# The second half of the up projection as seven block products in place of eight, for 8 of 11 column pairs, with the weight sums made in DRAM

## What is computed

```python
n2 = rmsnorm(h, ln2)
up = n2 @ w_up                      # 544 x 1024 by 1024 x 5632
u, vv = up[..., :D_FF], up[..., D_FF:]      # D_FF = 2816
uc, conv_tail = causal_dwconv(u, conv_prev, conv_w, conv_b)
h = h + (jax.nn.gelu(uc, approximate=False) * vv) @ w_down
```

## Time and profile before

| | before |
|---|---|
| time, median of 3 runs | 845.98 us (844.97 to 847.61) |
| the profiled execution: its time / its span | 846.78 / 844.7 us |
| busy: PE / DVE / ACT / POOL | 831.9 / 535.4 / 375.9 / 182.4 us |
| chain that ended last, share on PE | 93% |
| up loop on the chain | 453.3 to 712.6 us |

### The profile page before, as it was taken

One profiled execution on the slowest core, in us unless ns is written; L12 is line 12 of the kernel. 1 busy time (PEld: TensorE's weight loads), 2 busy tenths in 40 slices (PEclk: granted clock), 3 DMA queues, 4 the chain that ended last, 5 costly groups with the idle time before them and its releaser, 6 DMA issues.

```text
span 844.7 us, 16289 instructions
## 1 busy us (share of the span) xinstructions
PE 831.9 (98%) x6634; PEld 820.7 (97%) x6634; DVE 535.4 (63%) x671; ACT 375.9 (45%) x479; POOL 182.4 (22%) x224
## 2 busy tenths in 40 slices
PE   9999999999999999999999999999999999999996
PEld 8999999999999989999999999999999999999996
DVE  4464668486899876766555544545544555778973
ACT  5553234332455454543243533443443344644574
POOL 3017236343324200000400422222212122000020
PEclk9999999999999999999999999999999999999998
DMA  8769978982326993544892662232123323655522
GB/s 262 215 200 176 280 241 179 228 271 91 124 79 130 195 224 114 175 137 151 219 213 93 151 185 80 69 99 96 53 99 99 99 71 98 217 172 171 171 71 106
DMA packets 138526, 128.94 MB, mean 153 GB/s; under 512 B 5493, under 2 KB 130121, under 8 KB 138460
## 3 DMA queue, kind: packets, MB, share of 16 engines
q1 hardware_dynamic: 106636, 97.15, 37.1%
q0 software_dynamic: 31680, 30.55, 20.2%
q10 hardware_dynamic: 160, 0.53, 0.2%
HBM read 122.24 MB, written 41.62 MB: 194 GB/s over the span
## 4 chain that ended last, share of the span: by engine, by line
PE 93%; DVE 4%; ACT 1%; issue 1%; DMA 0%; DVEq 0%; SPq 0%; ACTq 0%
PE mm L1844 63%; PE mm L2235 8%; PE ax L1863 6%; PE ax L2235 6%; PE mm L2135 4%; PE ax L2135 3%; PE ax L1868 2%; DVE grs L1306 1%; DVE wlo L1296 1%; PE mm L1856 0%; ACT nhi L907 0%; DVE ylo L1541 0%; PE mm L1863 0%; DMA x_smp<-in_x_sample 0%; DVE wlo L1553 0%
## 5 line engine op out<-in xcount | busy, mean ns | idle before, releaser
L1844 PE MATMUL mm<-nhi,whi 128*128 128x272 f32 x1216 | 257.0, 293 | 0.9 <-DVE wlo L1296 0.6
L1844 PE MATMUL mm<-nhi,wlo 128*128 128x272 f32 x1216 | 252.8, 289 | 0.0
L1844 PE MATMUL mm<-nlo,whi 128*128 128x272 f32 x1216 | 251.8, 289 | 0.0
L1844 PEld LDWEIGHTS mm<-nhi,whi 128*128 128x128 f32 x1216 | 193.0, 190 | 3.5 <-issue 1.0
L1844 PEld LDWEIGHTS mm<-nlo,whi 128*128 128x128 f32 x1216 | 192.2, 190 | 0.0
L1844 PEld LDWEIGHTS mm<-nhi,wlo 128*128 128x128 f32 x1216 | 191.0, 190 | 0.0
L907 ACT ACTIVATE whi<-raw 128x2048 fp32r<-128x2048 f32 (+2 forms) x79 | 114.3, 1465 | 93.0 <-PE mm L1844 69.3
L1296 DVE TENSOR_TENSOR wlo<-raw,whi 128x2048 fp32r<-128x2048 f32 x44 | 103.7, 2356 | 28.7 <-ACT whi L907 28.6
L907 ACT ACTIVATE whi<-ring 128x1408 fp32r<-128x1408 f32 x25 | 34.6, 1383 | 44.1 <-PE ax L2235 24.0
L907 ACT ACT_TABLE_LOAD x22 | 28.2, 1283 | 58.3 <-DVE ext L1683 56.7
L2235 PE MATMUL mm<-bhi,whi 128*128 128x272 f32 x176 | 51.4, 292 | 0.0
(11 more groups left out here) (351 smaller groups left out, 1556.3 us busy)
## 6 DMA issues: line engine op xcount, KB each, us to landing
raw<-in_w_up SPq DMA_DIRECT2D x44, 512.0 KB, 4.4
raw<-in_w_in SPq DMA_DIRECT2D x36, 512.0 KB, 5.2
ring<-w_sums SPq DMA_DIRECT2D x16, 704.0 KB, 4.1
w_sums<-in_w_down SPq DMA_DIRECT2D x12, 704.0 KB, 11.4
w_sums<-in_w_down POOLq DMA_DIRECT2D x12, 704.0 KB, 16.7
ring<-in_w_down SPq DMA_DIRECT2D x9, 704.0 KB, 4.6
w_sums<-w_sums POOLq DMA_DIRECT2D x8, 704.0 KB, 9.5
g_sums<-in_w_in SPq DMA_DIRECT2D x18, 256.0 KB, 5.3
```

The costliest lines, as they stand in the source:

```text
L1844: ins = pe.matmul(mm[:, 2 * j + a, 0:HALF], w, x[:, kx, HALF * a:HALF * (a + 1)], start=first and n == 0 and m == 0, stop=last and n == le ...
```

## The change

Pairs 1 to 8 compute their v unit as `four` and `three`, seven block products in the four banks of `ax` (`UPS`, `UP_BLOCKS`); pairs 0, 9 and 10 stay as they were. The weight sums for it (`v_sums`, 256 KB a piece) are copied by SP in the last head units, where the copies for `w_sums` were, and added by POOL behind the head: 16 additions, 2 copies, 16 additions. SP waits for all of them before it loads the first `four`. The 12 copies for `w_sums` move to SP's loads of `w_o` and of u units 0 to 3, two at a time, and POOL's additions to the pauses behind pairs 0 to 7. The loops are written out. Token sums (`usum`, `uhigh`, `ulow`) are made around pairs 0 and 1. The last product takes its sign in the multiplication with the gelu. Two small shifts touch the gate units: in an `out` unit ACT copies `m_kept` of the next block before the second `mhi`, and `t_low(3)` comes after the second `mlo`.

The core of the diff:

```diff
+UPS = []
+for _i in range(KF // 2):
+    UPS += [("u", _i)] + ([("four", _i), ("three", _i)] if 1 <= _i <= 8 else [("v", _i)])
+U_DOWN = U_UP + len(UPS)
+UP_BLOCKS = range(1, 9)
...
+            if u >= 9:
+                i, block = gs_copies[(u - 9) // 2]
+                for n in range(1 + 4 * ((u - 9) % 2), 5 + 4 * ((u - 9) % 2)):
+                    sp.dma_start(v_sum(i, n), v_block(*block, n)).then_inc(vs_begun[i], 16)
...
+        for n, (kind, i) in enumerate(UPS):
+            u = U_UP + n
+            if kind in ("u", "v"):
+                load(u % 2, u - 1, *cols(w_up, UC * i + (D_FF if kind == "v" else 0)))
             else:
+                if i == 1:
+                    for k in (G_1, G_2, G_3) if kind == "four" else (G_4,):
+                        sp.wait_ge(vs_done[k], 16 * len(UP_BLOCKS))
+                block_load(u, kind, w_up, D_FF + UC * i, v_sums[:, i - 1])
+            if kind == "u" and i < 4:
+                begin_sums(2 + i)
...
+        for i in range(KF // 2):
             up_pair(i)
+            if i < 2:
+                weight_sum(S_3, (2 * i, 2 * i + 1), (0, 1))
+            elif i < 4:
+                weight_sum(S_1, (2 * i - 4, 2 * i - 3), (1, 1))
+            elif i < 6:
+                if i == 4:
+                    pool.wait_ge(sum_done[S_3], 16 * MD)
+                    for m in range(MD):
+                        pool.dma_start(w_sums[S_2, :, m], w_sums[S_3, :, m]).then_inc(sum_begun[S_2], 16)
+                else:
+                    weight_sum(S_2, (0, 1), (1, 1))
+            elif i == 6:
+                weight_sum(S_2, (2, 3), (1, 1))
+            elif i == 7:
+                pool.wait_ge(sum_done[S_2], 16 * MD)
+                weight_sum(S_4, range(MD), S_2)
...
+        for k in range(4):
+            run(tile(usum[0], k), resid[:, k, HALVES[1]], ACT.Copy, t_first, scale=vec(V_LN2 + k))
+        for i in range(KF // 2):
...
+                if j == 1 and i in UP_BLOCKS:
+                    keep(gact[:, 2 * i, HALVES[0]], ax, b, 0)
                 if j == 1:
...
+                    next_hi(x)
+                if j == 1 and i in UP_BLOCKS:
+                    keep(gact[:, 2 * i + 1, HALVES[1]], ax, b, 1)
...
+        make_sums(usum, V_LN2, 0)
         inverse(rstd[:, :], "rstd2", rstd_ready)
...
+            if kind in ("u", "v"):
                 for j in range(2):
...
+            elif kind == "four":
+                if i == 1:
+                    aux_wait_drained(pe, "rstd2")
+                four(u, up_block(i), ax, uhigh, ulow, 4)
+            else:
+                three(u, up_block(i), ax, uhigh, ulow, 4)
```

More of the change, by code:

```diff
@@ L432, in build @@
     silu_done, y_prod, y_hi, y_lo = map(sem, ("silu_done", "y_prod", "y_hi", "y_lo"))
+    vs_begun = [sem(f"vs_begun{i}") for i in range(4)]
+    vs_done = [sem(f"vs_done{i}") for i in range(4)]
     gs_begun = [sem(f"gs_begun{i}") for i in range(4)]
@@ L508, in flat, with gate_kind, first_piece @@
         return t[:, :, :].rearrange("p k c -> p (k c)")
+    def gate_kind(u):
+        return GATES[u - U_GATE][0] if U_GATE <= u < U_WO else UPS[u - U_UP][0] if U_UP <= u < U_DOWN else None
+    PIECED = [u for u in range(U_BLOCK, U_DOWN) if u < U_WO or gate_kind(u) in ("four", "three")
+              or gate_kind(u) and gate_kind(u - 2) == "four"]
     def pieces(u):
-        return (slice(0, 512), slice(512, 1536)) if GATES[u - U_GATE][0] == "three" else (slice(0, 1024), slice(1024, 2048))
+        return (slice(0, 512), slice(512, 1536)) if gate_kind(u) == "three" else (slice(0, 1024), slice(1024, 2048))
+    def first_piece(u):
+        return PIECED.index(u) + 1
     def blocks(g, q):
@@ L1118, in _ @@
                         next_hi(u)
+                        if q < 3:
+                            keep(m_kept[:, :], ax, blocks(0, q + 1)[1], 0)
                     act.wait_ge(m_sum, 2 * q + j + 1)
@@ L1127, in _ @@
                     act.wait_ge(block_added, 4 * blocks(g, q)[1] - 1)
-                keep(m_kept, g, q, 0)
+                    keep(m_kept[:, :], (ax, mm)[g], blocks(g, q)[1], 0)
                 if g == 0:
@@ L1596, in _ @@
                         dve.wait_ge(s0r_out[i], 32)
-                    make_sums(0)
-                    make_sums(1)
+                    make_sums(tsum, V_LN1, 0)
+                    make_sums(tsum, V_LN1, 1)
                     next_lo(u)
                 else:
-                    t_low(0)
-                    t_low(1)
+                    t_low(tsum, tlow, thigh, 0)
+                    t_low(tsum, tlow, thigh, 1)
             elif kind == "out":
@@ L1612, in _ @@
                             next_lo(u - 1)
-                        if q == 0 and b == 1 and j == 1:
-                            t_low(3)
                         dve.tensor_tensor(halves(mx[b][:, :]), slot(b), halves(gsig[:, 2 * b + j, :]), ALU.mult
@@ L1621, in _ @@
                     dve.tensor_tensor(mlo[:, m, :], mx[0][:, :], mhi[:, m, :].bitcast(F32), ALU.subtract).then_inc(m_lo, 1)
-                    if q == 0 and j == 0:
-                        t_low(2)
+                    if q == 0:
+                        t_low(tsum, tlow, thigh, 2 + j)
                 next_lo(u)
@@ L1714, in up_pair @@
-            u = U_UP + 1
-            lo(u + 2, u % 2, i * 2 + (u + 3))
-        with dve.Fori(0, KH // 2 + 1) as i:
+                        k = i * 2 - KH - 1
+                        third(gact[:, k:k + 2, HALVES[0]], gact[:, i * 2 - 1:i * 2 + 1, HALVES[0]])
+            next_lo(x + (2 if blocked else 1))
+            if i == 0:
+                make_sums(usum, V_LN2, 3)
+                t_low(usum, ulow, uhigh, 0)
+        for i in range(KF // 2):
             up_pair(i)
-        st.n -= 6
@@ L2112, in _, with block_product @@
                           done=filled_sem(s) if j == NJ - 1 else None)
-        def block_product(u, g, q, product, first, step, xh, xl):
-            n, b = blocks(g, q)
+        def block_product(u, b, bank_of, product, first, step, xh, xl):
             s = u % 2
             start = product not in (2, 4, 6)
-            if b >= 2 and product == 0:
-                pe.wait_ge(block_kept, 3 * (b - 2) + 3)
-            elif b >= 2 and start:
-                pe.wait_ge(block_added, 4 * (b - 2) + {1: 2, 3: 4, 5: 3}[product])
+            last = b - 2 if b < 6 else b - 1
+            if start and last >= 0:
+                pe.wait_ge(block_kept, 3 * last + 3)
+                if product:
+                    pe.wait_ge(block_added, 4 * last + {1: 2, 3: 4, 5: 3}[product])
             if product == 2:
@@ L2129, in block_product @@
                 pe.wait_ge(block_added, 4 * b + 1)
-            out = (ax, mm)[g][:, BLOCK_BANKS[product], 0:HALF]
+            out = bank_of[:, BLOCK_BANKS[product], 0:HALF]
             for k in range(4):
```

402 lines of the change are left out of this document (242 added, 160 removed).

## The result

| | before | after |
|---|---|---|
| time, median | 845.98 us (844.86 to 849.31, 7 runs) | 850.03 us (849.48 to 853.11, 7 runs) |
| ratio to before | | 1.0046, 95% interval 1.0033 to 1.0059 |
| the profiled execution: its time / its span | 846.78 / 844.7 us | 849.79 / 848.0 us |

The change makes the kernel slower by 4 us, where 842 us was forecast; the time lies inside the range of 836 to 851, on the wrong side of the kernel before.

A forecast was written before the change was run, and what follows sets the result against it. PE was taken to bound the kernel. From 846.78 us, -12.0 matmuls, -1.6 `m_kept`, +6.4 start, +2.0 loads and +1.0 gates gave 842.6, stated as 842 for the median; range 836 to 851.

The forecast's parts named there:

- The matmuls, -12.0: Up loop: eight pairs lose 12 matmuls each, 96 at 0.1252 us, 12.0 us less.
- The start, +6.4: Start of the up loop: four new waits of PE, 1.5, 1.5, 2.1 and 1.3 us, together 6.4, bounds 4.5 to 8.
- the start costs nothing: Rival, start of the up loop: the sums hide behind matmuls after all, giving 835.5 us; chance 0.12.
- A steady pair, at nothing: Block pairs of the up loop: PE's 22.5 us hide the other engines' work, cost zero; `keep` has half a microsecond left.
- `m_kept`, -1.6: Gates, first block's third product: the earlier copy removes PE's 2.0 us wait; gain 1.6 us, between 0 and 2.0.
- The gates ... 1.0 us, bounds 0 and 3: Gates: longer POOL additions may delay the load of the second gate's `three`, with `m_kept` behind it; cost 1.0 us.
- The loads ... I put 2.0 us on this: Up loop: POOL's additions may delay loads, around pairs 2 and 3 and behind pair 7; cost 2.0 us, bounds 0 and 12.
- The rival that it ends slower: Up loop: loads become the bound, the next `four` landing 10.2 us after release in each block pair; 852 us, chance 0.15.
- an even share, some 9 us: Loads beside additions: queues taking turns by packet would give SP's load every second turn, no wait, 2.0 us less.
- the row of 16.5 us: Profile row before the change: a pair of loads lands in 16.5 us beside four additions, 4.3 in quiet.

The follow-up runs named there:

- Experiment 10: Changed kernel with S_4's additions later, second half of v additions in `w_o` stage, token sums early, SP's copies out of `w_o`: 832.59 us, 0.9825.
- Experiments 4 and 5: Changed kernel with token sums made earlier: 844.55 us; second version, first two `ulow` behind pair 0's first multiplication by the gelu: 842.52 us.
- experiment 3: Changed kernel, POOL holding the second half of the v additions until the gates end: 843.06 us, 0.9945.
- experiment 1: Kernel before with only the two small shifts in the gate units: 845.33 us, 0.9972.
- experiment 4: Changed kernel with token sums made earlier, first version, the first two `ulow` ahead of the multiplication by the gelu: 844.55 us, 0.9963.
- experiment 8: Changed kernel, additions for down in fours: 852.13 us; S_4's late, S_1's four behind pair 7: 854.4 us; S_4's two each behind pairs 7 and 8: 846.52 us.
- The three cures together: Changed kernel with S_4's additions behind pairs 8 and 9, second half of v additions in `w_o` stage, token sums early: 832.0 us, 0.9819.

## Why the prediction was wrong

The stages give the sum of the changed kernel, from the head's end to down, 455.72 - 451.65 = +4.1 us. Its parts are -12.0 for the matmuls, -2.0 for `m_kept`'s first wait, +6.65 for the additions in the gates, +6.4 start, +0.8 pair 2, +4.0 pair 8, and +0.2 in hundredths over the other pairs, together +4.05. The forecast had -4.2 for the same sum; two steps failed, the gates and the loads.

- **The matmuls, -12.0: right.** A block unit of the loop takes 10.55 us. Experiment 10, with no wait, has the up loop at 699.34 - 450.55 = 248.8 us against 260.24, 11.4 less; of the 0.6 that is missing 0.3 lie in pair 0 (19.32 us, before 19.00), the rest in hundredths over the others.
- **The start, +6.4: right in its four waits and their places; in its sum partly by luck.** The waits are 1.3, 2.0, 0.7 and 0.8 us, where 1.5, 1.5, 2.1 and 1.3 were forecast, so 4.8 and not 6.4. Behind each of them PE takes another 0.3 us to come back to its pace, at the full clock, and two shorter halts ahead of products cost 0.5; the prediction had neither. Experiments 4 and 5 took it away by placing alone; the rival "the start costs nothing" describes their kernel, not the changed one.
- **A steady pair, at nothing: right.** Pairs 3 to 7 wait for nothing, and `keep` is on time.
- **`m_kept`, -1.6: the mechanism right,** and with the later loads in quiet it is worth 2.0 (experiment 3).
- **"The gates ... 1.0 us, bounds 0 and 3": this step failed.** It came to 6.65 us. I had the right victim (the second gate's `three`, with `m_kept` behind it) and the right cause (POOL's additions lasting beyond 300 us), and priced it with the landings of 5.8 and 9.8. The load in question took 8.6 us, within those; what it cost PE was mis-sized. Its packets took turns with those of the additions (1329 to 1321 from 309 to 317 us). What I left out is that the 5.8 us of room were shortened by the very gain of 2.0 at `m_kept`, which brings PE sooner (experiment 1 shows this in quiet, 0.6 us), that ACT and `m_kept` come 1.5 us after the landing, and that PE restarts at half its clock, 1.8 us.
- **"The loads ... I put 2.0 us on this": mis-sized.** It came to 4.0 us at pair 8 and 0.8 at pair 2, whose `four` landed 9.7 us after its issue. I had named pair 8 and its four additions, but priced them with 13.9 us, under the 14.5 that the load had. That figure is the median landing of the four additions, not that of a load beside them; the load took 17.9, and the earlier trace rows had 16.5 for a load beside such additions. And again the clock: 2.3 us of wait, 1.8 us of matmuls at 1.2 GHz.
- **The rival that it ends slower** foresaw loads of 10.2 us in each pair. The `four` landed in 4.5 to 5 us in most pairs, as its additions start behind it, and in 6.3 to 9.7 in pairs 2, 3 and 5. It ended slower by another way: two waits of a few microseconds, dear ones.

The prediction took turns between queues for an even share, some 9 us, and held that the row of 16.5 us contradicts it. The turns are there, and it was the even share that failed: packets went 217 to 218, but the additions' packets had 5.5 times the bytes and took seven times as long, so the load had a sixth of the bytes (0.22 of 1.35 MB). The rule of the Trainium skill, "DMA: Bandwidth & Descriptors", section "Queues, rings and completion order", that a DMA engine changes between its queues a packet at a time, agrees with all these traces. Nor is it the order of issue: in the gates the load issued at 304.12 us landed at 312.7, ahead of two additions that POOL had issued at 302.70 and 303.45 us (315.1 and 318.0).

What stays open: why the clock fell at a wait of 1.9 us (experiment 4) and not at 1.8, 1.6 or at the 2.0 at the start of the up loop. Whether S_4's additions in packets of 0.5 KB would leave pair 8 without a wait, as S_1's did in experiment 8, was not tried. The head's scatter of 3 us was not looked into.

## What to carry to other kernels

When transfers are moved, price a load by the packets that are in flight beside it on other queues, by their number and by how long one takes, not by bandwidth or by the landing of the transfers themselves: keep bursts small and put them right behind the load that can least wait. A gain at one wait shortens the room of the next one, so the sum of a change must carry the new arrival times on. And work that is free on average (here four sums of tokens) costs its length where it stands between a result and the engine that waits for it; the same instructions some units earlier cost 0.3 us. The three cures together turned 1.0046 into 0.9819.

## What the runs showed of the hardware

- A wait of TensorE costs more than its length: after 4.3 and 2.3 us (and once 1.9) it ran at 0.50 of its clock, 1.2 GHz, for some 3.5 us, 1.8 us more; after 1.6 and 1.8 us, and after 2.0 at the start of the up loop, the granted clock stayed at 1.00 and it lost 0.25 to 0.3.
- Four accumulating DMAs of 704 KB from DRAM to DRAM, issued within 3.4 us beside the loads of the loop, landed 8.8, 12.9, 16.2 and 19.6 us after their own issue.
- The queues of SP and POOL took turns packet by packet (217 to 218, 327 to 327, 967 to 982). A load with packets of 1 KB (0.06 us each) moved some 380 KB per us alone, 160 beside additions with packets of 0.5 KB (0.06 us) and some 36 beside additions with packets of 5.5 KB (0.44 us).
- SP, which issues a half load in 0.4 to 0.5 us, also beside four additions (641.46 us), took 3.8 to 6.7 us for one behind its own two copies while POOL's accumulating DMAs were in flight, and 7.9 to 8.5 for two copies of 704 KB that take 2.5 in quiet. Its queue is then late as a whole.
